# Expert weights as 16 KB runs in 8 ring slots, with the tokens' columns gathered in the same order

## What is computed

```python
def ec_moe(u, w_router, w_gate, w_up, w_down):      # 16 experts, 64 tokens each
    cap = (EC_CAPACITY_FACTOR * T) // N_EXPERTS
    aff = jax.nn.softmax((u @ w_router).astype(jnp.float32), axis=-1)
    gates, idx = lax.top_k(jnp.swapaxes(aff, 1, 2), cap)
    xs = u[bidx, idx]
    hid = jax.nn.silu(jnp.einsum('becd,edf->becf', xs, w_gate)) * jnp.einsum('becd,edf->becf', xs, w_up)
    ys = jnp.einsum('becf,efd->becd', hid, w_down) * gates[..., None].astype(u.dtype)
    return jnp.zeros_like(u).at[bidx, idx].add(ys)
```

## Time and profile before

| | |
|---|---|
| runs of the kernel | 2462.3, 2459.29, 2460.76 us; median 2460.76 |
| profiled execution | 2459.52 us, its span 2457.7, granted clock 0.971 of full speed |
| TensorE, VectorE, ScalarE, GpSimd busy | 2245.1, 1015.8, 623.8, 236.1 us |
| DMA | 577.89 MB, 235 GB/s on the mean |
| issues of expert pieces | 384 of 1 MB, some 21 to 23 us from issue to landing |

### The profile page before, as it was taken

One profiled execution on the slowest core, in us unless ns is written; L12 is line 12 of the kernel. 1 busy time (PEld: TensorE's weight loads), 2 busy tenths in 40 slices (PEclk: granted clock), 3 DMA queues, 4 the chain that ended last, 5 costly groups with the idle time before them and its releaser, 6 DMA issues. The chain is left out here.

```text
span 2457.7 us, 31444 instructions
## 1 busy us (share of the span) xinstructions
PE 2245.1 (91%) x12140; PEld 1496.1 (61%) x12140; DVE 1015.8 (41%) x1810; ACT 623.8 (25%) x1304; POOL 236.1 (10%) x285
## 2 busy tenths in 40 slices
PE   3998989889977999999899999998899989999999
PEld 2777668579965444343434343433677778787877
DVE  3578634645664111211111111112764664664355
ACT  4342223344432110110101010100343341333321
POOL 4223333810010000000000000000000000000000
PEclk8999999999987999999999999999999999999999
DMA  6113655754555999999999999998322105331131
GB/s 235 52 52 121 222 186 183 206 134 123 155 188 204 417 424 424 425 425 425 425 425 426 425 425 426 425 425 359 123 86 69 36 22 184 125 97 60 51 130 59
DMA packets 214256, 577.89 MB, mean 235 GB/s; under 512 B 65945, under 2 KB 100738, under 8 KB 180482
## 3 DMA queue, kind: packets, MB, share of 16 engines
q1 hardware_dynamic: 205976, 563.13, 59.5%
q0 software_dynamic: 2496, 8.40, 1.1%
q10 hardware_dynamic: 5673, 4.83, 0.6%
HBM read 543.81 MB, written 32.51 MB: 234 GB/s over the span
## 5 line engine op out<-in xcount | busy, mean ns | idle before, releaser
L1833 PE MATMUL ps_gate_up<-expert_ring,pair_columns 128*64 128x512 f32 x1024 | 457.8, 600 | 49.7 <-DMA expert_ring<-in_moe_w_up_dram 42.5
L1834 PE MATMUL ps_gate_up<-expert_ring,pair_columns 128*64 128x512 f32 x1024 | 458.9, 601 | 0.0
L1833 PEld LDWEIGHTS ps_gate_up<-expert_ring,pair_columns 128*64 128x64 f32 x1024 | 136.2, 138 | 331.5 <-issue 328.9
L120 PE MATMUL second_bank<-stream_high,columns_high 128*128 128x512 f32 x640 | 264.9, 414 | 10.8 <-PEq L92 6.8
L122 PE MATMUL second_bank<-stream_high,columns_low 128*128 128x512 f32 x640 | 251.6, 393 | 0.0
L121 PE MATMUL second_bank<-stream_low,columns_high 128*128 128x512 f32 x640 | 251.5, 393 | 0.0
L2139 DVE TENSOR_TENSOR hidden_tokens<-silu_gate,ps_gate_up 64x512 f32<-64x512 f32 x64 | 42.3, 690 | 500.2 <-ACT silu_gate L2020 499.7
L1820 PE MATMUL ps_down<-expert_ring,hidden_columns 128*64 128x512 f32 x512 | 227.0, 596 | 0.0
L1821 PE MATMUL ps_down<-expert_ring,hidden_columns 128*64 128x512 f32 x512 | 227.0, 595 | 0.0
L1820 PEld LDWEIGHTS ps_down<-expert_ring,hidden_columns 128*64 128x64 f32 x512 | 67.3, 137 | 130.7 <-issue 123.6
L120 PEld LDWEIGHTS second_bank<-stream_high,columns_high 128*128 128x128 f32 x640 | 121.5, 190 | 41.5 <-issue 15.3
(11 more groups left out here) (536 smaller groups left out, 3805.2 us busy)
## 6 DMA issues: line engine op xcount, KB each, us to landing
expert_ring<-in_moe_w_gate_dram SPq DMA_DIRECT2D x128, 1024.0 KB, 21.7
expert_ring<-in_moe_w_up_dram SPq DMA_DIRECT2D x128, 1024.0 KB, 23.4
expert_ring<-in_moe_w_down_dram SPq DMA_DIRECT2D x128, 1024.0 KB, 20.8
win_ring<-in_gdn_w_in_dram SPq DMA_DIRECT2D x16, 1024.0 KB, 8.6
late_mod_ring<-in_w_mod_dram SPq DMA_DIRECT2D x16, 1024.0 KB, 5.7
stream_raw<-in_w_in_even_dram SPq DMA_DIRECT2D x16, 1024.0 KB, 5.8
stream_raw<-in_w_in_odd_dram SPq DMA_DIRECT2D x16, 1024.0 KB, 5.3
stream_raw<-in_w_ple_gate_dram SPq DMA_DIRECT2D x8, 1024.0 KB, 10.8
```

The source lines that it names most:

```text
L120: nc.tensor.matmul(out, sh, mh, start=start, stop=False)
L1833: mm(psA[LO, c], xe[:, e, k], ex.gate_up[s0][:, j, cols], start=(k == 0), stop=(k == KC - 1))
L1834: last = mm(psA[HI, c], xe[:, e, k], ex.gate_up[s1][:, j, cols], start=(k == 0), stop=(k == KC - 1))
```

## The change

A piece becomes 2 MB and a slot 16 KB per partition; the ring has 8 slots and the same size. Partition p now holds two neighbouring channels of gate or up (of each 256, channels 2p and 2p + 1), or four neighbouring hidden units of down (of each 512), so that a partition's part of a piece is one run of 16 KB in memory. An expert has 12 pieces and 4 gate-and-up groups of 16 matmuls each, which free two slots at their end.

Because channels and units now lie in another order over the partitions, the matmuls against them need their other operand in that order. The gathers read every second column of `xn` (`row_tokens`), the turns every fourth of the hidden values (`units`), and scale and bias per channel are brought into that order once, by 8 small matmuls against every second column of the identity (`spread_columns`, in the output projection after its second step), which VectorE copies into `row_columns`. In the first pair the next two columns are gathered in the middle of each group, after two of its four chunks, and group kr waits for columns 2 kr and 2 kr + 1.

```diff
 class ExpertRing:
-    SLOTS, ROWS, DOWN_ROWS = 16, 1, 2
+    SLOTS, ROWS, DOWN_ROWS = 8, 2, 4
...
-        self.wg, self.wu = (dram[n][0].rearrange("e (k p) f -> p e k f", p=P) for n in ("moe_w_gate", "moe_w_up"))
-        self.wd = dram["moe_w_down"][0].rearrange("e (q r p) d -> p e q r d", p=P, r=self.DOWN_ROWS)
+        self.wg, self.wu = (dram[n][0].rearrange("e (b p r) f -> p e b (r f)", p=P, r=self.ROWS) for n in ("moe_w_gate", "moe_w_up"))
+        self.wd = dram["moe_w_down"][0].rearrange("e (q p r) d -> p e q (r d)", p=P, r=self.DOWN_ROWS)
...
-                for n in range(HALVES):
-                    sp.wait_ge(w_low, n + 1)
-                    ex.fill(sp, w_out.SLOT + n)
+                for n in range(HALVES // 2):
+                    sp.wait_ge(w_low, 2 * n + 2)
+                    ex.fill(sp, w_out.SLOT // 2 + n)
                 sp.wait_ge(done, LT)
-                for n in (0, 1):
-                    ex.fill(sp, n)
+                ex.fill(sp, 0)
                 sp.wait_ge(done, 2 * LT)
-                for n in (4, 5, *range(w_out.SLOT + HALVES, ex.SLOTS)):
+                for n in (2, 5, 6, 7):
                     ex.fill(sp, n)
                 sp.wait_ge(logits, 1)
-                for n in (2, 3):
-                    ex.fill(sp, n)
+                ex.fill(sp, 1)
...
+                def spread_columns():
+                    pe.wait_ge(scaled_ready, 2)
+                    for i, x in enumerate((scale, bias)):
+                        for r in range(ROWS):
+                            one_hot = ident.rearrange("p (n r) -> p r n", r=ROWS)[:, r]
+                            for half, part in enumerate((LO, HI)):
+                                chunks = x.rearrange("p (b a) -> p a b", a=ROWS)[:, half]
+                                last = nc.tensor.matmul(spread_bank[part, i, r], one_hot, chunks, start=True, stop=True)
+                    last.then_inc(columns_spread, 1)
+
                 def turn_tokens(t):
+                    if t == 0:
+                        pe.wait_ge(columns_kept, 1)
...
+                row_tokens = lambda t, k: xn[:, t].rearrange("p (b n r) -> p b r n", b=GROUPS, r=ROWS)[:, k // ROWS, k % ROWS]
...
-                        last = mm(turn_of(bank, j), xn[:, t, k * P:(k + 1) * P], sel[:, t].rearrange("p e c -> p (e c)"),
+                        last = mm(turn_of(bank, j), row_tokens(t, k), sel[:, t].rearrange("p e c -> p (e c)"),
...
+                    units = hid[HI, c % 2].rearrange("p (q n r) -> p q r n", n=P, r=DOWN_ROWS)
                     for j in range(4):
-                        last = mm(psT[:, c % 2, j], hid[HI, c % 2, j * P:(j + 1) * P],
-                                  ident[HI, HI], start=True, stop=True)
+                        last = mm(psT[:, c % 2, j], units[:, j // DOWN_ROWS, j % DOWN_ROWS], ident[HI, HI], start=True, stop=True)
...
-                def gate_up(g, at, e, kr):
+                def gate_up(g, at, e, kr, between=()):
...
+                        if c == CHUNKS // 2 - 1:
+                            for k in between:
+                                gather_first(k)
                     last.then_inc(taken, 1)
...
+                        def gate_up_of(kr):
+                            if first and e == 0:
+                                pe.wait_ge(first_staged, ROWS * (kr + 1))
+                                gate_up(g, at, e, kr, range(ROWS * (kr + 1), min(ROWS * (kr + 2), KC)))
+                            else:
+                                gate_up(g, at, e, kr)
...
-                                                    scale=scale[:, k:k + 1], bias=bias[:, k:k + 1])
+                                                    scale=row_scale[k], bias=row_bias[k])
...
+                        dve.wait_ge(columns_spread, 1)
+                        nc.vector.tensor_copy(row_columns[:, :, :, :], spread_bank).then_inc(columns_kept, 1)
```

More of the change, by code:

```diff
@@ L1556, in __init__ @@
         self.slot = [m.sem(f"piece_loaded{i}") for i in range(self.SLOTS)]
-        place = [ring[:, i] for i in range(self.SLOTS)]
-        self.gate_up = [x.rearrange("p (k n) -> p k n", n=DFF) for x in place]
-        self.down = [x.rearrange("p (r d) -> p r d", d=D) for x in place]
-        self.wg, self.wu = (dram[n][0].rearrange("e (k p) f -> p e k f", p=P) for n in ("moe_w_gate", "moe_w_up"))
-        self.wd = dram["moe_w_down"][0].rearrange("e (q r p) d -> p e q r d", p=P, r=self.DOWN_ROWS)
+        self.place = [ring[:, i] for i in range(self.SLOTS)]
+        self.gate_up = [x.rearrange("p (r n) -> p r n", n=DFF) for x in self.place]
+        self.down = [x.rearrange("p (r d) -> p r d", d=D) for x in self.place]
+        self.wg, self.wu = (dram[n][0].rearrange("e (b p r) f -> p e b (r f)", p=P, r=self.ROWS) for n in ("moe_w_gate", "moe_w_up"))
+        self.wd = dram["moe_w_down"][0].rearrange("e (q p r) d -> p e q (r d)", p=P, r=self.DOWN_ROWS)
     def load(self, sp, g, n):
@@ L1567, in load @@
         if i < 2 * self.GROUPS:
[L1568 to L1572 removed]
+            src = (self.wg, self.wu)[i % 2][:, ex, i // 2].rearrange("p a n -> p (a n)")
+        else:
+            src = self.wd[:, ex, i - 2 * self.GROUPS].rearrange("p a n -> p (a n)")
         last_of = self.PIECES - self.SLOTS + i
@@ L1691, in output_and_experts @@
         first_bank = lambda k: ps_row[:, k % 2]
+        columns_spread, columns_kept = m.sem("ffn_columns_spread"), m.sem("ffn_row_columns_kept")
+        spread_bank = psD[:, 0, 0:2 * KC].rearrange("p (i r b) -> p i r b", i=2, r=ROWS)
+        row_scale, row_bias = ([row_columns[:, i, k % ROWS, k // ROWS:k // ROWS + 1] for k in range(KC)] for i in range(2))
         next_bank = [ps_row[:, 0], ps_row[:, 1], psD[:, 0], psD[:, 1]]
@@ L1759, in _ @@
                         rows(1, 5)
+                    if n == 2:
+                        spread_columns()
                     i, t = n // LT, n % LT
@@ L1848, in pair @@
                         pe.wait_ge(hidden, at * CHUNKS + CHUNKS)
-                        for kr in range(GROUPS // 2):
-                            if first and e == 0:
-                                pe.wait_ge(first_staged, kr + 1)
-                            gate_up(g, at, e, kr)
-                            if first and e == 0:
-                                gather_first(kr + 2)
+                        def gate_up_of(kr):
[4 more added lines that the diff above has]
+                                gate_up(g, at, e, kr)
+                        for kr in range(GROUPS // 2):
+                            gate_up_of(kr)
                         if e == 0:
@@ L1862, in pair @@
                             gather(0, psD[:, 0])
-                        for kr in range(GROUPS // 2, GROUPS - 2):
-                            if first and e == 0:
-                                pe.wait_ge(first_staged, kr + 1)
-                            gate_up(g, at, e, kr)
-                            if first and e == 0:
-                                gather_first(kr + 2)
+                        for kr in range(GROUPS // 2, GROUPS - 1):
+                            gate_up_of(kr)
                         if e and more:
@@ L1871, in pair @@
                             gather(1, psD[:, 0])
-                        for kr in range(GROUPS - 2, GROUPS):
-                            if first and e == 0:
-                                pe.wait_ge(first_staged, kr + 1)
-                            gate_up(g, at, e, kr)
+                        gate_up_of(GROUPS - 1)
                         turn(at, 0)
```

12 lines of the change are left out of this document (6 added, 6 removed).

## The result

The changed kernel takes 2513.03 us (median of 4 runs, 2511.37 to 2521.35), the kernel before beside it 2460.16. The ratio is 1.0228, 95% interval 1.0216 to 1.024: 53 us slower. The profiled execution is one of 2511.66 us, its span 2509.9, granted clock 0.952 (0.971 before).

A forecast was written before the change was run, and what follows sets the result against it. The prediction took the expert stage to be bound by its DMA stream, with 47 us of slack on TensorE. Terms -13.3 + 6.1 + 3.5 + 1.5 = -2.2 us gave 2457.3, or 2458.5 by the median; range 2453 to 2465.

The forecast's parts named there:

- The strided weight loads: Gathers loading every second column and turns every fourth hidden unit on TensorE: taken as free, between free and twice as long.
- the rival: Strided loads twice as long: turns' 512 records add 55 us on TensorE, time 2470; chance 0.19.
- the room: Time TensorE's turns could lose before they set the stage's end: 43 us, or 84 ns on each record.
- signs of being wrong: Rate above 434 or below 428 GB/s; turns over 3.3 us; rate dipping near 913; stage not ending with the stream.
- 872.8: Expert stage: us TensorE would need if no piece were late, 920.2 less 47.4 of waits.
- The rate: Expert weight stream: 16 KB packets at 608 ns take 895.0 us instead of 908.3, 13.3 us less.
- The start: First reload of the expert stream comes 6.1 us later: 0.65 wait for both columns, 3.42 another row, 2.05 two gathers.
- The small matmuls: Eight matmuls put into the output projection, where TensorE is full: 1.5 us more, bounds 0 and 1.9.
- The end: After the last up piece TensorE needs 25.0 us, the stream 19.5; the stage ends 3.5 us later than now.
- The queue: Reload pause at the first pair's end: 3.1 us of cover remain; rival of dry queue or cut runs, chance 0.10.
- The sum: All terms against the profiled execution: -2.2 us, so 2457.3, or 2458.5 by the median; chance as summed 0.50.

The follow-up runs named there:

- ordered: The changed kernel, but VectorE writes the hidden values in the down weights' order so turns load 128 neighbouring columns again; 2457.78 us, ratio 1.0.
- step2: The changed kernel with a 2 MB down piece as two runs of 8 KB per partition, so turns load every second hidden unit; 2461.65 us, ratio 1.0018.
- twice_apart: The kernel before with every turn computed twice and the third and fourth chunks' turns parted by down matmuls; 2501.41 us, ratio 1.0178.
- turn_twice: The kernel before with each turn computed twice in succession, loads contiguous; 2491.7 us, ratio 1.0134.
- ladder: The kernel before with the four turns of each chunk loading every 1st, 2nd, 3rd and 4th hidden value; 2463.59 us in one execution.

## Why the prediction was wrong, step by step

**The strided weight loads: the step that failed.** "Between free and twice as long I take free" was wrong for the turns: the sum has no term for them. A load at 16 bytes takes 325 ns and not 188, and a record came every 3.95 / 16 = 0.247 us and not every 0.12. That is +62.8 us on TensorE, where the rival had 55 and the room was 43. One of the prediction's own signs of being wrong, turns over 3.3 us, thus came. For the gathers, at 8 bytes, it was right (196 against 192 ns, +2.8 us in 448 records). The reason given, that two unlike sources take the same, compared two contiguous loads and said nothing about a step.

**The rival had half of the mechanism.** It forecast 2470, about 10 us more; it was 2513, 53 more. Its price for the loads was nearly right (55 us for 62.8), but a second step failed in forecast and rival alike: both took the clock as it was. The doubled blocks of turns leave TensorE at half clock in 24 of 32 cases, which costs 44 us on matmuls that the change doesn't touch. 872.8 + 62.8 + 44.0 + 2.8 - 10.2 = 972.2 us, and the stage measured 972.8. The -10.2 comes from the waits that are gone, since the 872.8 counted as work what they brought with them. Three waits of 2.9 to 3.0 us in the trace of before have gate and up records at half clock behind them, of which this is the first:

```profile
1296.97 1.04 PE L1833 MATMUL ps_gate_up<-expert_ring,pair_columns 128*64 128x512 f32 x1 [2.92 <-DMA expert_ring<-in_moe_w_up_dram]
```

With the start of the stage such records are 27, an estimated 6 us of the 10 (13 to 14 pairs at 0.43 us each), and the mean of all is 600 ns where it is 594 now. The rest fits the restarts, an estimated 0.15 us after each of 29 waits.

**The rate was right.** 12 us of the changed stage (1204 to 1216) have 352 packets, 37 of them small: 16 x 12 / 315 = 609.5 ns; 12 us from 1276 on give 16 x 12 / 316 = 607.6, for the 608 taken.

```profile
DMA packets 352, 5.16 MB, mean 430 GB/s; under 512 B 37, under 2 KB 37, under 8 KB 37
```

In ordered, where the stream is the bound again, the first reload to the last down matmul is 1709.53 - 802.24 = 907.3 us; 916.1 - 13.3 + 3.5 = 906.3 was the prediction's sum.

**The start was right in sum.** The first reload, at 796.62, is 9.58 us behind the first gate matmul (4.12 before); the prediction's figures give 799.8 - 790.2 = 9.6:

```profile
787.04 0.61 PE L1847 MATMUL ps_gate_up<-expert_ring,pair_columns 128*64 128x512 f32 x1 [0.71 <-issue]
```
```profile
796.62 0.93 SPq L1581 DMA_DIRECT2D expert_ring<-in_moe_w_down_dram  x2
```

The absolute time is 3.2 us early because this execution was 3.2 us ahead already where the output projection begins (684.34 against 687.54); from there to the first gate matmul is 102.70 us against 100.51, +2.2, for 0.65 + 1.5. The parts are not, so the agreement of the sum is in part luck. The small matmuls take 0.58 us of TensorE (716.27 to 716.85), not 1.5, and the wait for both columns 0.71. The other 0.9 us were not tied to the change: from the output projection to the first gather the mean granted clock is 0.79 here and 0.82 before, and the output projection's records are 5 to 10 ns longer. In ordered, with the same code at the start, six pairs ran at half clock and the first reload came 12.12 us behind the first gate matmul; the prediction has no such term either.

```profile
716.27 0.41 PE L1734 MATMUL ps_down<-ffn_scale,identity_and_ones 128*64 128x4 f32 x8
716.54 0.39 PE L1734 MATMUL ps_down<-mod_columns,identity_and_ones 128*64 128x4 f32 x8
716.85 0.50 PE L120 MATMUL ps_gate_up<-gdn_w_out_high,o_columns_high 128*128 128x512 f32 x1
```

**The end was right, where the stream bounds.** In step2 the last group starts when its piece lands (1679.42) and the last down matmul ends 25.2 us later; 25.0 was taken. In the changed kernel nothing waits at the end, so the term doesn't apply.

**The queue.** It never lacked a cover in ordered and step2 (422 to 434 GB/s in every stretch of 20 us or more that was read between 820 and 1690 us). In the changed kernel the stream pauses at each pair (200 GB/s from 1285 to 1295 us) while SP waits for slots that TensorE frees too late, which is the new bound and not that rival.

**The sum.** Without the turns it said -2.2 us; ordered measured -0.5 with an interval of -2.5 to +2.2, and step2, with 3.1 us more of stream, +3.6 (2.2 to 6.6). The longer runs in memory thus gained nothing that these times can tell, even without their price. What 16 KB packets give at the rate (13 us) goes ahead of the stage (2.2 us, of which 1.3 were found) and at its two ends (5.5 and some 3.5 us), where a piece of 2 MB makes both the first free slot and the last group later.

**What stays open.** How often the clock falls differs between kernels with blocks of the same length (14 of 16, 15 of 32, 24 of 32, 29 of 32), so the table orders them but doesn't price them; and why they differ is open. twice_apart is 10 us slower than turn_twice; by their traces only 959.4 - 954.6 = 4.8 us of it lie in the stage, and the other 4.9 before its first gate matmul and behind its last down matmul, where no edit reaches. That the fall goes with long turn blocks is shown, with fast loads and with slow ones; what about them brings it (their few columns, their width of 64) wasn't tried.

## What to carry to other kernels

A new layout in memory is paid where the other operand is read: before a strided weight load is taken as free, measure one, since here 8 bytes were nearly free and 16 bytes cost 70% a load. An engine's slack has to hold the clock's answer as well as the added work: blocks of small matmuls that went from 2 to 4 us took 62.8 us more themselves and cost 44 us on the large ones behind them. And larger pieces move a stream's start and end by a piece each; count both against the gain in rate before anything else.

## What the runs showed of the hardware

- A float32 weight load of 64 rows and 128 columns takes 186, 193, 254 and 320 ns (medians, in ladder) at steps of 4, 8, 12 and 16 bytes.
- TensorE's clock fell to 1.2 GHz at blocks of 16 to 32 turn records that last 3.8 us or more, though not at each (24 of 32 in after), and at 6 of ladder's 32 of 2.7 us (mean granted clock 0.66 to 0.86 in stretches of 4 us in which TensorE was busy for 4.00), and some 3 to 7 pairs of down records behind them ran at it. Blocks of gathers of 3.8 to 4.0 us, 32 records with 128 columns, had no slower records behind them: in before and after all 28 are followed by 32 gate and up records in 7.1 us.
- VectorE's product of 64 x 512 values takes 1064 ns and not 690 when its output is written in steps of 512 bytes, its inputs read in order as before (ordered).
- A DMA packet of 16 KB takes 608 to 610 ns (after), beside 307 for 8 KB and 155.7 for 4 KB (before).
